# Three 256-column matmuls per weight tile in place of a 512- and a 256-column one, in a two-layer float32 transformer kernel

## The chip, the cores and the metric

One core of one Trainium2 chip. The metric is the device time of one launch in microseconds (us), the median of several runs.

## What is computed

Two layers over 256 tokens of 2048 channels, batch 1, all in float32. Each layer normalises, runs a mixer and adds it to the residual stream `h`, then normalises, runs a squared-ReLU MLP and adds that; a last norm follows. Cut to what matters here:

```python
# layer 0: even_mixer, layer 1: odd_mixer
hn  = rms_norm(h, norm_mix[layer])
h   = h + mixer(hn)          # hn @ w_in -> attention / recurrence -> @ w_out
hn  = rms_norm(h, norm_mlp[layer])
h   = h + jnp.square(jax.nn.relu(hn @ w_up[layer])) @ w_down[layer]
# at the end
out = rms_norm(h, final_norm)
```

The weights are 2048 x 3584 (even in), 2048 x 2048 (even out), 2048 x 6144 (odd in), 2048 x 2048 (odd out), and for each layer's MLP 2048 x 8192 and 8192 x 2048. Nearly all the work is these products.

## The kernel before, in words

**Split operands.** Every operand of a large product is held as a sum of two parts in the type float32r: a high part (a float32r copy) and a low part (the value minus that copy). The product then is high x high + high x low + low x high. For activations the two parts lie side by side in one row of `hg_op` (the normed stream) or `ff_op` (the mixer's or MLP's inner activations): columns 0 to 255 (S = 256 tokens) hold the high part, 256 to 511 the low one.

**Weights.** A weight slice of 512 rows x 256 columns (512 KB, [128, 4, 256] in SBUF) is one *sub*. `load_quad` (L327) has SyncE load a sub into one of four `raw` slots as soon as VectorE is done with the slot (`lo_done`). ScalarE makes the high part (`split_hi`, L338, the copy is L346), VectorE the low part (`split_lo`, L348, the subtraction is L353), both `AHEAD` = 3 subs ahead of TensorE, into one of four `w_split` slots.

**Quads.** Eight subs make a *quad*: 512 output columns as two groups of 256, each over the 2048 rows in four subs. There are 91 quads, so 728 subs. A quad's four output tiles of 128 channels x 256 tokens lie in PSUM banks 0 to 3, one tile a bank. `quad_pe` (L516) runs `pe_sub` (L355) for each sub: for each of the 2 output tiles and each of 4 row tiles it issues two matmuls (L374), so 8 pairs a sub, 5,824 pairs in all:

- "hi": weight tile high x the full 512-column row of the activations. High x high adds into columns 0 to 255 of the bank, high x low into columns 256 to 511 (the *cross half*).
- "lo": weight tile low x the 256 high columns, added into columns 0 to 255.

Each matmul is recorded as two instructions, a weight load (128 x 128, the row PEld) and the matmul. The order is lo, hi, but hi, lo for the first row tile of an output tile; so at row tiles 0 and 1 two 256-column matmuls stand side by side. Four quads of the odd mixer's input (its values, tokens on the partitions) go through `pe_sub_tok` (L381), where the activations are the stationary operand and the weights move; the same two widths, L401.

**Leaving PSUM.** `quad_split` (L523) is the order written out for ScalarE and VectorE: at each place 0 to 7 of a quad one split, and after the splits of places 4 and 7 (6 and 7 in quads with a late order) the group that is done *leaves*. First ScalarE waits for the tile (`pe_count`) and copies the cross half to SBUF (`act_cross`, L409, the copy is L412), then VectorE adds the main half to it into `total` (`dve_total`, L414, the add is L417) and frees the bank (`bank_free`). Then VectorE uses `total`: `residual` (L437) adds it into `h` (L463), `hidden` (L472) takes ReLU times the norm's factor (L485), `projected` (L492) scales it (L500). ScalarE and VectorE then make the next high and low parts. `projected_tok` (L502) folds the add into its scaling. TensorE waits for `bank_free` at the first sub of a group before it writes the bank again.

**Between them**, hooks of `stage_hook` put the attention, the recurrence, the norms and the final transposes at fixed places of the quads, on banks 4 to 7. VectorE's `h_ready` and `proj_done` tell them when `h` or a projection is there; `v_pe_stage` has TensorE transpose the first projection at place 2 of quad 1.

Of the kernel before, what the change touches and what calls it, by code (L numbers as in the profile page):

```python
# [36 lines left out]
P = 128  # L37
# [4 lines left out]
KT = 16  # L42
# [53 lines left out]
def build(nc, x, rel_bias, norm_mix, even_w_in, even_conv_w, even_conv_b, even_gate_a_w, even_gate_a_b,  # L96
# [30 lines left out]
    with ctx:  # L127
# [13 lines left out]
        cross = sb("cross", [P, 4, S])  # L141
        total = sb("total", [P, 4, S])
# [80 lines left out]
        cross_done = sem("cross_done")  # L223
        bank_free = sem("bank_free")
        relu_done = sem("relu_done")
# [10 lines left out]
        proj_done = sem("proj_done")  # L236
# [70 lines left out]
        R_EVEN_OUT, R_MLP0 = 0, 4  # L307
        R_ODD_OUT, R_MLP1 = 4 + 4 * CHUNKS, 8 + 4 * CHUNKS
# [46 lines left out]
        def pe_sub(pe, Q, s, pos, op, ready, base, first):  # L355

            g, kq = s // 4, s % 4
            slot = pos % SPLIT_SLOTS
            pe.wait_ge(lo_done, 8 * Q + pos + 1)
            if first:  # L360

                n = SUB_KT * (kq + 1)
                pe.wait_ge(ready, even_out_tiles(n) if isinstance(Q, int) and Q == Q_EVEN_OUT else base + n)
            for j in range(2):
                i = 2 * g + j
                if kq == 0 and not (isinstance(Q, int) and Q == 0):

                    pe.wait_ge(bank_free, 4 * Q - 4 + i + 1)
                for kt in range(SUB_KT):
                    k = SUB_KT * kq + kt  # L370
                    hi = (psum[:, i, 0:2 * S], w_hi[:, slot, kt, j * P:(j + 1) * P], op[:, k, :])
                    lo = (psum[:, i, 0:S], w_lo[:, slot, kt, j * P:(j + 1) * P], op[:, k, 0:S])
                    for n, (o, l, r) in enumerate((hi, lo) if k == 0 else (lo, hi)):
                        ins = nc.tensor.matmul(o, l, r, start=(k == 0 and n == 0), stop=(k == KT - 1 and n == 1),  # L374
                                               skip_group_check=True)
                if kq == 3:
                    ins.then_inc(pe_count, 1)
            if kq < 3:
                ins.then_inc(pe_count, 1)

        def pe_sub_tok(pe, Q, s, pos, op, ready, base, first):  # L381
# [8 lines left out]
            for tb in range(TB):  # L390
                i = 2 * g + tb
                if kq == 0:

                    pe.wait_ge(bank_free, 4 * Q - 4 + i + 1)
                both = psum[:, i].rearrange("p (a c) -> p a c", a=2)
                for kt in range(SUB_KT):
                    k = SUB_KT * kq + kt
                    hi = (both, op[:, k, tb * P:(tb + 1) * P], w_split[:, slot, :, kt, :])
                    lo = (both[:, 1], op[:, k, S + tb * P:S + (tb + 1) * P], w_hi[:, slot, kt, :])
                    for n, (o, l, r) in enumerate((hi, lo) if k == 0 else (lo, hi)):  # L400
                        ins = nc.tensor.matmul(o, l, r, start=(k == 0 and n == 0), stop=(k == KT - 1 and n == 1),  # L401
                                               skip_group_check=True)
                if kq == 3:
                    ins.then_inc(pe_count, 1)
# [14 lines left out]
        def act_prep(act, nrm, n, i, src_ready, col):  # L419

            act.wait_ge(h_ready, src_ready)
# [15 lines left out]
        def residual(which, eng, Q, g, R, n0, prep):  # L437
# [5 lines left out]
            if which == "act":  # L443
                act_cross(eng, Q, g)
                for i in tiles:
                    if last:
                        eng.wait_ge(h_ready, KT + 4 * R + i + 1)
                        eng.activation(sq[:, i], tile(h, n0 + i, 0, S), ACT.Square).then_inc(prep_done, 1)
                    elif prep:
                        act_prep(eng, prep[0], n0 + i, i, KT + 4 * R + i + 1, prep[1])  # L450
# [21 lines left out]
        def hidden(which, eng, Q, g, U, n0):  # L472

            if which == "act":
                act_cross(eng, Q, g)
                for i in (2 * g, 2 * g + 1):
                    eng.wait_ge(relu_done, 4 * U + i + 1)
# [4 lines left out]
            dve_total(eng, Q, g)  # L482
# [9 lines left out]
        def projected(which, eng, Q, g, dst, scale):  # L492

            if which == "act":
                act_cross(eng, Q, g)
                return
            dve_total(eng, Q, g)
            for i in (2 * g, 2 * g + 1):
                eng.wait_ge(bank_free, 4 * Q + i + 1)
                eng.scalar_tensor_tensor(dst(i), total[:, i], scale, rstd, ALU.mult, ALU.mult).then_inc(proj_done, 1)  # L500

        def projected_tok(which, eng, Q, g, c0):  # L502

            for tb in range(TB):
                i, r = 2 * g + tb, rstd_tok[:, tb:tb + 1]
                if which == "act":
                    eng.wait_ge(pe_count, after_tile(Q, i))
                    eng.wait_ge(rstd_done, 2 + 1)
                    eng.activation(cross[:, i], psum[:, i, S:2 * S], ACT.Copy, scale=r).then_inc(cross_done, 1)
                else:  # L510
                    eng.wait_ge(cross_done, 4 * Q + i + 1)
                    eng.scalar_tensor_tensor(v_tok[:, tb, c0:c0 + GC], psum[:, i, 0:S], r, cross[:, i],
                                             ALU.mult, ALU.add).then_inc(bank_free, 1)
# [282 lines left out]
        def kpad_act(act):  # L796
            act.wait_ge(proj_done, 2)
# [6 lines left out]
        def v_pe_stage(pe):  # L804
            pe.wait_ge(proj_done, 4)
# [17 lines left out]
        def swa_qk_pe(pe, g):  # L823
            key = SWA_FIRST[g]
            pe.wait_ge(proj_done, 4 * (1 + g // 2) + 2 * (g % 2) + 2)
# [114 lines left out]
        def lru_conv_dve(dve, m, taps):  # L940
            if taps[0] == 3:
                p0 = 4 * (3 + m // 2) + 2 * (m % 2)
                dve.wait_ge(proj_done, p0 + 2)
# [72 lines left out]
        def lru_out_act(act, m):  # L1016
            act.wait_ge(proj_done, 4 * (5 + m // 2) + 2 * (m % 2) + 2)
# [59 lines left out]
        def even_in_leave(Q):  # L1077
            q = Q - Q_EVEN_IN

            def leave(which, eng, g):  # L1080
# [12 lines left out]
                elif q <= 4:  # L1093
                    if which == "dve" and q == 3 and g == 0:
                        eng.memset(xpad[:, :, 0:3], 0.0).then_inc(dve_seq, 1)
                        seq["dve"] += 1
                        eng.wait_ge(dve_seq, seq["dve"])

# [13 lines left out]
        def z_pe(pe, n):  # L1112
            i = n % 4
            pe.wait_ge(proj_done, 4 * (7 + 4 + n // 4) + i + 1)
# [112 lines left out]
        def mixer_out(which, eng, w, Q0, R0, base, nrm, first_quad, key0):  # L1227
            for n in range(4):
                def leave(which, eng, g, n=n):
                    residual(which, eng, Q0 + n, g, R0 + n, 4 * n, (nrm, norm_cols[nrm]))  # L1230
# [3 lines left out]
        def mlp(which, eng, layer, Q0, R0, A0, nrm):  # L1234
# [10 lines left out]
            def down(c, g, prep=None, until=8, hook=None):  # L1245
                Q = Q0 + 8 * c + 4 + g
                run_quad(which, eng, Q, wd, D * c, 512 * g, ff_op, ff_ready, A0 + KT * c + 0,
                         lambda which, eng, grp: residual(which, eng, Q, grp, R0 + 4 * c + g, 4 * g, prep),
# [27 lines left out]
        def program(which, eng):  # L1276
            mixer_in(which, eng, w_even_in, Q_EVEN_IN, EVEN_IN_COLS, even_in_leave, 0, 0)
            mixer_out(which, eng, w_even_out, Q_EVEN_OUT, R_EVEN_OUT, A_EVEN, 1, Q_EVEN_IN, 0)
            mlp(which, eng, 0, Q_MLP0, R_MLP0, A_MLP0, 1)
            mixer_in(which, eng, w_odd_in, Q_ODD_IN, ODD_IN_COLS, odd_in_leave, 2, ODD)  # L1280
            mixer_out(which, eng, w_odd_out, Q_ODD_OUT, R_ODD_OUT, A_ODD, 3, Q_ODD_IN, ODD)
            mlp(which, eng, 1, Q_MLP1, R_MLP1, A_MLP1, 3)
# [155 lines left out]
```

## Time and profile before

| | |
|---|---|
| median of 3 runs | 2204.99 us (2204.65 to 2206.67) |
| the profiled execution, span from first to last instruction | 2204.3 us |
| the profiled execution's own time beside its span | not shown apart; the median of the runs is 0.7 us over the span |
| TensorE busy | 2147.9 us, 97% |
| TensorE weight loads busy | 1864.1 us, 85% |
| VectorE busy | 1328.2 us, 60% |
| ScalarE busy | 1139.4 us, 52% |
| granted TensorE clock, mean | 0.989 |
| moved by DMA | 392.83 MB, 178 GB/s |

A matmul's recorded duration includes the way through the array, and the records of neighbours overlap, so a duration isn't what the matmul costs. What it costs is the time from its start to the next one's: the length of an unbroken stretch over the number of matmuls in it.

### The profile page before, as it was taken

The page shows a single profiled execution, that of the slowest core. Times are in us where ns is not written, and L with a number is a line of the kernel's source. Part 1 is how long each engine was busy: PE and PEld are TensorE (multiplying, and loading weights), DVE is VectorE, ACT ScalarE, POOL GpSimd, SP SyncE. Part 2 cuts the span into 40 slices and gives each one's busy share as a digit, 9 for nine tenths or more (in the row PEclk, how much of TensorE's full clock was granted, in tenths as well). Part 3 has the DMA queues.
Part 4 walks back from the last instruction along what each step waited for, and adds up shares of the span by engine and source line. Part 5 has one row for each costly group of instructions (what it writes and reads, how often), then busy time and mean ns, then how long its engine had stood idle before and what let it go on. Part 6 is the DMA issues. An engine that isn't in the chain of part 4 may idle for free.

```text
span 2204.3 us, 34808 instructions
## 1 busy us (share of the span) xinstructions
PE 2147.9 (97%) x12170; PEld 1864.1 (85%) x12170; DVE 1328.2 (60%) x1873; ACT 1139.4 (52%) x1761; POOL 59.3 (3%) x91
## 2 busy tenths in 40 slices
PE   7499999999999999999999999999999999999998
PEld 6388888888888888888888888888888888888887
DVE  6268776655655665666655555676556656655664
ACT  4258855544544544555444466555445544544555
POOL 5011100000000000000000000000000000000000
PEclk9699999999999999999999999999999999999999
DMA  7854556566666566565555544556666656565653
GB/s 183 158 173 134 164 183 183 181 195 186 186 186 186 180 193 184 181 191 186 185 185 188 186 140 134 161 177 188 191 184 188 189 183 185 183 191 176 196 182 124
DMA packets 391821, 392.83 MB, mean 178 GB/s; under 512 B 15744, under 2 KB 388624, under 8 KB 391744
## 3 DMA queue, kind: packets, MB, share of 16 engines
q1 hardware_dynamic: 387552, 385.99, 56.7%
q0 software_dynamic: 3584, 5.79, 2.0%
q8 instruction: 48, 0.79, 0.2%
q14 instruction: 29, 0.24, 0.0%
q10 hardware_dynamic: 608, 0.03, 0.0%
HBM read 386.49 MB, written 5.24 MB: 178 GB/s over the span
## 4 chain that ended last, share of the span: by engine, by line
PE 95%; DMA 2%; ACT 1%; SPq 1%; DVE 0%; POOL 0%; issue 0%; ACTq 0%; DVEq 0%; POOLq 0%
PE psum L374 87%; PE psum L401 4%; DMA raw<-in_even_w_in_dram 2%; PE psum L837 0%; PE psum L1121 0%; POOL relu_sq L891 0%; PE psum L1147 0%; PE psum L1163 0%; PE psum L971 0%; PE psum L834 0%; SPq L579 0%; PE psum L1149 0%; DVE w_split L353 0%; PE psum L1165 0%; PE psum L1148 0%
## 5 line engine op out<-in xcount | busy, mean ns | idle before, releaser
L353 DVE TENSOR_TENSOR w_split<-raw,w_split 128x1024 fp32r<-128x1024 f32 x728 | 885.9, 1228 | 688.6 <-ACT w_split L346 684.5
L346 ACT ACTIVATE w_split<-raw 128x1024 fp32r<-128x1024 f32 x728 | 762.6, 1056 | 767.8 <-PE psum L374 679.8
L374 PE MATMUL psum<-hg_op,w_split 128*128 128x512 f32 (+1 forms) x6016 | 1078.0, 341 | 18.4 <-DVE w_split L353 18.1
L374 PEld LDWEIGHTS psum<-hg_op,w_split 128*128 128x128 f32 x6016 | 927.4, 189 | 158.8 <-DVE w_split L353 18.9
L374 PE MATMUL psum<-ff_op,w_split 128*128 128x512 f32 (+1 forms) x5120 | 907.1, 340 | 0.0
L374 PEld LDWEIGHTS psum<-ff_op,w_split 128*128 128x128 f32 x5120 | 785.1, 188 | 117.6
L412 ACT ACTIVATE cross<-psum 128x256 f32<-128x256 f32 x348 | 122.2, 377 | 124.6 <-PE psum L374 124.5
L417 DVE TENSOR_TENSOR total<-psum,cross 128x256 f32<-128x256 f32 x348 | 138.0, 418 | 58.8 <-ACT cross L412 58.6
L478 ACT ACTIVATE relu_sq<-relu_sq 128x256 f32<-128x256 f32 x128 | 52.5, 410 | 82.7 <-DVE relu_sq L485 82.7
L401 PE MATMUL psum<-w_split,hg_op 128*128 128x512 f32 (+1 forms) x512 | 90.7, 340 | 0.0
L401 PEld LDWEIGHTS psum<-w_split,hg_op 128*128 128x128 f32 x512 | 78.5, 188 | 11.8
L488 DVE TENSOR_TENSOR ff_op<-relu_sq,ff_op 128x256 f32 (+1 forms) x128 | 54.5, 426 | 54.4 <-ACT ff_op L479 52.6
L463 DVE TENSOR_TENSOR h<-h,total 128x256 f32 (+1 forms) x160 | 59.9, 416 | 0.1
L479 ACT ACTIVATE ff_op<-relu_sq 128x256 f32 (+1 forms) x128 | 51.4, 402 | 0.0
L485 DVE SCALAR_TENSOR_TENSOR relu_sq<-total,rstd 128x256 f32<-128x256 f32 x128 | 47.9, 416 | 0.0
L422 ACT ACTIVATE relu_sq<-h 128x256 f32<-128x256 f32 (+1 forms) x48 | 19.7, 410 | 31.9 <-DVE h L463 31.9
L432 DVE TENSOR_TENSOR ssq<-ssq,relu_sq 128x256 f32<-128x256 f32 x48 | 20.2, 421 | 14.7 <-ACT hg_op L423 14.7
L423 ACT ACTIVATE hg_op<-h,pcol 128x256 fp32r<-128x256 f32 (+1 forms) x48 | 23.7, 495 | 0.0
L500 DVE SCALAR_TENSOR_TENSOR mix<-total,rstd 128x256 f32<-128x256 f32 x60 | 23.7, 436 | 0.0
L433 DVE SCALAR_TENSOR_TENSOR hg_op<-h,pcol,hg_op 128x256 fp32r<-128x256 f32 (+1 forms) x48 | 22.9, 478 | 0.0
L834 PE MATMUL psum<-mix 128*128 128x128 f32 x32 | 5.3, 319 | 13.3 <-DVE mix L500 13.2
L1139 DVE SCALAR_TENSOR_TENSOR mix<-psum,mix 128x384 f32<-128x384 f32 x16 | 8.9, 558 | 14.4 <-ACT mix L1134 14.4
(150 smaller groups left out, 535.5 us busy)
## 6 DMA issues: line engine op xcount, KB each, us to landing
raw<-in_w_up_dram SPq DMA_DIRECT2D x256, 512.0 KB, 3.9
raw<-in_w_down_dram SPq DMA_DIRECT2D x256, 512.0 KB, 3.6
raw<-in_odd_w_in_dram SPq DMA_DIRECT2D x96, 512.0 KB, 3.5
raw<-in_even_w_in_dram SPq DMA_DIRECT2D x56, 512.0 KB, 4.4
raw<-in_even_w_out_dram SPq DMA_DIRECT2D x32, 512.0 KB, 4.3
raw<-in_odd_w_out_dram SPq DMA_DIRECT2D x32, 512.0 KB, 3.7
rel_dram<-mix POOLq DMA_DIRECT2D x4, 768.0 KB, 37.7
mix<-in_x_dram SPq DMA_DIRECT2D x4, 512.0 KB, 8.3
```

Of the source, the lines that this page charges most:

```text
L346: act.activation(w_hi[:, slot], raw[:, rs], ACT.Copy).then_inc(hi_done, 1)
L353: dve.tensor_tensor(w_lo[:, slot], raw[:, rs], w_hi[:, slot].bitcast(F32), ALU.subtract).then_inc(lo_done, 1)
L374: ins = nc.tensor.matmul(o, l, r, start=(k == 0 and n == 0), stop=(k == KT - 1 and n == 1), skip_group_check=True)
L401: ins = nc.tensor.matmul(o, l, r, start=(k == 0 and n == 0), stop=(k == KT - 1 and n == 1), skip_group_check=True)
L412: act.activation(cross[:, i], psum[:, i, S:2 * S], ACT.Copy).then_inc(cross_done, 1)
L417: dve.tensor_tensor(total[:, i], psum[:, i, 0:S], cross[:, i], ALU.add).then_inc(bank_free, 1)
L423: act.activation(tile(hg_op, n, 0, S), tile(h, n, 0, S), ACT.Copy, scale=pcol[:, 0, one(col + n)]).then_inc(prep_done, 1)
L463: eng.tensor_tensor(dst, dst, total[:, i], ALU.add).then_inc(h_ready, 1)
L478: eng.activation(sq[:, i], relu[:, i], ACT.Square).then_inc(sq_done, 1)
L479: eng.activation(tile(ff_op, n0 + i, 0, S), relu[:, i], ACT.Square).then_inc(sq_done, 1)
L485: eng.scalar_tensor_tensor(relu[:, i], total[:, i], 0.0, rstd, ALU.max, ALU.mult).then_inc(relu_done, 1)
L488: eng.tensor_tensor(tile(ff_op, n0 + i, S, 2 * S), sq[:, i], tile(ff_op, n0 + i, 0, S).bitcast(F32), ALU.subtract).then_inc(ff_ready, 1)
```

## The change

In `pe_sub` and `pe_sub_tok` the 512-column matmul becomes two of 256 columns that load the same stationary tile again, and all three of a row tile add into columns 0 to 255 of the bank. The cross half, the copy of it by ScalarE and the add by VectorE are gone, with the buffers `cross` and `total`. VectorE waits for `pe_count` itself and reads PSUM where it read `total`; `bank_free` is now signalled by that consumer and takes the place of `h_ready`, `relu_done` and `proj_done` for those who waited for them. `projected_tok` becomes one scaling on VectorE. One wait is new in the even mixer: before VectorE writes `xpad` again it waits for the convolution, which it runs itself.

```diff
@@ pe_sub
+                acc = psum[:, i, 0:S]
                 for kt in range(SUB_KT):
                     k = SUB_KT * kq + kt
-                    hi = (psum[:, i, 0:2 * S], w_hi[:, slot, kt, j * P:(j + 1) * P], op[:, k, :])
-                    lo = (psum[:, i, 0:S], w_lo[:, slot, kt, j * P:(j + 1) * P], op[:, k, 0:S])
-                    for n, (o, l, r) in enumerate((hi, lo) if k == 0 else (lo, hi)):
-                        ins = nc.tensor.matmul(o, l, r, start=(k == 0 and n == 0), stop=(k == KT - 1 and n == 1),
-                                               skip_group_check=True)
+                    wh, wl = w_hi[:, slot, kt, j * P:(j + 1) * P], w_lo[:, slot, kt, j * P:(j + 1) * P]
+                    nc.tensor.matmul(acc, wl, op[:, k, 0:S], start=(k == 0), stop=False)
+                    nc.tensor.matmul(acc, wh, op[:, k, S:2 * S], start=False, stop=False)
+                    ins = nc.tensor.matmul(acc, wh, op[:, k, 0:S], start=False, stop=(k == KT - 1))
@@ pe_sub_tok
-                both = psum[:, i].rearrange("p (a c) -> p a c", a=2)
+                acc = psum[:, i, 0:GC]
-                    hi = (both, op[:, k, tb * P:(tb + 1) * P], w_split[:, slot, :, kt, :])
-                    lo = (both[:, 1], op[:, k, S + tb * P:S + (tb + 1) * P], w_hi[:, slot, kt, :])
+                    ah, al = op[:, k, tb * P:(tb + 1) * P], op[:, k, S + tb * P:S + (tb + 1) * P]
+                    nc.tensor.matmul(acc, al, w_hi[:, slot, kt, :], start=(k == 0), stop=False)
+                    nc.tensor.matmul(acc, ah, w_lo[:, slot, kt, :], start=False, stop=False)
+                    ins = nc.tensor.matmul(acc, ah, w_hi[:, slot, kt, :], start=False, stop=(k == KT - 1))
@@ gone
-        def act_cross(act, Q, g):
-            for i in (2 * g, 2 * g + 1):
-                act.wait_ge(pe_count, after_tile(Q, i))
-                act.activation(cross[:, i], psum[:, i, S:2 * S], ACT.Copy).then_inc(cross_done, 1)
-        def dve_total(dve, Q, g):
-            for i in (2 * g, 2 * g + 1):
-                dve.wait_ge(cross_done, 4 * Q + i + 1)
-                dve.tensor_tensor(total[:, i], psum[:, i, 0:S], cross[:, i], ALU.add).then_inc(bank_free, 1)
@@ residual, VectorE
-            dve_total(eng, Q, g)
             for i in tiles:
-                eng.wait_ge(bank_free, 4 * Q + i + 1)
+                eng.wait_ge(pe_count, after_tile(Q, i))
                 dst = tile(h, n0 + i, 0, S)
-                eng.tensor_tensor(dst, dst, total[:, i], ALU.add).then_inc(h_ready, 1)
+                eng.tensor_tensor(dst, dst, psum[:, i, 0:S], ALU.add).then_inc(bank_free, 1)
@@ hidden, VectorE (projected likewise, with its own scaling)
-                eng.wait_ge(bank_free, 4 * Q + i + 1)
-                eng.scalar_tensor_tensor(relu[:, i], total[:, i], 0.0, rstd, ALU.max, ALU.mult).then_inc(relu_done, 1)
+                eng.wait_ge(pe_count, after_tile(Q, i))
+                eng.scalar_tensor_tensor(relu[:, i], psum[:, i, 0:S], 0.0, rstd, ALU.max, ALU.mult).then_inc(bank_free, 1)
@@ even_in_leave, VectorE, for xpad
+                        if q > 3 or g:
+                            eng.wait_ge(lru_xc, 2 * (2 * (q - 3) + g))
```

## Rows read from the trace of the kernel before

**Rows 1.** The page: busy time by engine, and the granted clock in 40 slices.

```profile
PE 2147.9 (97%) x12170; PEld 1864.1 (85%) x12170; DVE 1328.2 (60%) x1873; ACT 1139.4 (52%) x1761; POOL 59.3 (3%) x91
PEclk9699999999999999999999999999999999999999
```

**Rows 2.** Windows by stage: busy of each engine (instructions), clock, DMA share, GB/s.

```profile
core 0: us, PE busy (x) PEld busy (x) DVE busy (x) ACT busy (x) POOL busy (x), PEclk, DMA share, GB/s
0.00:100.00 100.00, 55.94 (x270) 47.55 (x271) 44.65 (x59) 38.05 (x60) 34.66 (x66) 0.80 0.84 180
350.00:1075.00 725.00, 725.00 (x4112) 629.78 (x4111) 441.11 (x612) 363.48 (x547) 0.00 (x0) 1.00 0.60 186
2192.50:2204.30 11.80, 1.42 (x9) 0.99 (x8) 4.07 (x11) 5.14 (x11) 0.00 (x0) 0.64 0.47 178
```

**Rows 3.** The chain of waits, 400 to 1060 us: start us, us, what.

```profile
399.94 660.29 PE psum L374 x3742
```

**Rows 4.** Groups of TensorE instructions by line and shape.

```profile
L374 PE MATMUL psum<-ff_op,w_split 128*128 128x512 f32 x2560 | 893.8, 398 | 0.0
L374 PE MATMUL psum<-ff_op,w_split 128*128 128x256 f32 x2560 | 693.6, 281 | 0.0
...
L374 PEld LDWEIGHTS psum<-ff_op,w_split 128*128 128x128 f32 x5120 | 785.1, 188 | 117.6
```

**Rows 5.** The chain of waits while the granted clock was 0.50, with that window.

```profile
33.61 4.27 PE psum L374 x13
...
33.82:37.68 3.86, 3.86 (x14) 3.26 (x13) 3.86 (x4) 1.20 (x2) 3.27 (x3) 0.50 0.73 223
```

**Rows 6.** Timeline at row tiles 0 and 1: matmuls 256, 256, 512; weight loads.

```profile
807.62 0.63 PE L374 MATMUL psum<-ff_op,w_split 128*128 128x256 f32 x3
...
807.62 0.30 PEld L374 LDWEIGHTS psum<-ff_op,w_split 128*128 128x128 f32 x2
...
807.74 0.31 PEld L374 LDWEIGHTS psum<-ff_op,w_split 128*128 128x128 f32 x2
```

**Rows 7.** Timeline at the end: four matmuls with a single moving column each.

```profile
2195.22 0.52 PEld L1328 LDWEIGHTS psum<-ones,ssq 128*128 128x128 f32 x4 [3.02 <-DVE ssq L468]
```

**Rows 8.** The chain of waits: plain float32 matmuls, 128 columns (L905), 512 columns (L915).

```profile
122.83 0.87 PE psum L905 x8
...
126.48 0.86 PE psum L915 x2
```

**Rows 9.** The page: groups of ScalarE and VectorE instructions that the change touches.

```profile
L412 ACT ACTIVATE cross<-psum 128x256 f32<-128x256 f32 x348 | 122.2, 377 | 124.6 <-PE psum L374 124.5
L417 DVE TENSOR_TENSOR total<-psum,cross 128x256 f32<-128x256 f32 x348 | 138.0, 418 | 58.8 <-ACT cross L412 58.6
...
L463 DVE TENSOR_TENSOR h<-h,total 128x256 f32 (+1 forms) x160 | 59.9, 416 | 0.1
```

**Rows 10.** Who waited for whom: line <- releaser: us, times, longest.

```profile
ACT w_split L346 <- PE psum L374: 679.8, 429, 7.7
...
PE psum L374 <- DVE w_split L353: 18.1, 2, 17.0
PE psum L834 <- DVE mix L500: 13.2, 1, 13.2
```

**Rows 11.** The chain of waits at the end of quad 0 and before L834.

```profile
45.13 0.39 ACT cross L412
45.52 0.02 issue
45.54 0.42 DVE total L417
45.97 0.67 DVE mix L500 x2
46.63 1.15 DVE w_split L353
...
47.80 40.82 DMA raw<-in_even_w_in_dram
...
92.86 0.67 DVE total L417 x2
93.53 0.68 DVE mix L500 x2
```

**Rows 12.** The chain of waits behind the last large matmul.

```profile
2189.74 2.80 PE psum L374 x16
2192.54 0.02 issue
2192.56 0.39 ACT cross L412
2192.95 0.02 issue
2192.98 0.42 DVE total L417
2193.40 0.34 DVE h L463
```

More of the change, by code:

```diff
@@ L140, in build @@
         ff_op = sb("ff_op", [P, KT, 2 * S], F32R)
-        cross = sb("cross", [P, 4, S])
-        total = sb("total", [P, 4, S])
         relu_sq = sb("relu_sq", [P, 8, S])
@@ L406, in pe_sub_tok, with act_prep @@
                 ins.then_inc(pe_count, 1)
[L409 to L421 removed]
+        def act_prep(act, nrm, n, i, count, col):
+            act.wait_ge(bank_free, count)
             act.activation(sq[:, i], tile(h, n, 0, S), ACT.Square).then_inc(prep_done, 1)
@@ L435, in dve_prep, with residual @@
                                      ALU.mult, ALU.subtract).then_inc(hg_ready, 1)
-        def residual(which, eng, Q, g, R, n0, prep):
+        def residual(which, eng, Q, g, n0, prep):
             tiles = (2 * g, 2 * g + 1)
@@ L494, in projected @@
             if which == "act":
-                act_cross(eng, Q, g)
                 return
-            dve_total(eng, Q, g)
             for i in (2 * g, 2 * g + 1):
-                eng.wait_ge(bank_free, 4 * Q + i + 1)
-                eng.scalar_tensor_tensor(dst(i), total[:, i], scale, rstd, ALU.mult, ALU.mult).then_inc(proj_done, 1)
+                eng.wait_ge(pe_count, after_tile(Q, i))
+                eng.scalar_tensor_tensor(dst(i), psum[:, i, 0:S], scale, rstd, ALU.mult, ALU.mult).then_inc(bank_free, 1)
         def projected_tok(which, eng, Q, g, c0):
+            if which == "act":
+                return
             for tb in range(TB):
                 i, r = 2 * g + tb, rstd_tok[:, tb:tb + 1]
[L506 to L513, printed above, removed]
+                eng.wait_ge(pe_count, after_tile(Q, i))
+                eng.wait_ge(rstd_done, 2 + 1)
+                eng.tensor_scalar(v_tok[:, tb, c0:c0 + GC], psum[:, i, 0:GC], r, None, ALU.mult).then_inc(bank_free, 1)
         def quad_pe(pe, Q, op, ready, base, hook=None):
@@ L804, in v_pe_stage @@
         def v_pe_stage(pe):
[L805 removed]
+            pe.wait_ge(bank_free, 4)
             for m in range(2):
@@ L1097, in leave @@
                         eng.wait_ge(dve_seq, seq["dve"])
+                    if which == "dve":
+                        if q > 3 or g:
+                            eng.wait_ge(lru_xc, 2 * (2 * (q - 3) + g))
                     def dst(i):
@@ L1247, in down @@
                 run_quad(which, eng, Q, wd, D * c, 512 * g, ff_op, ff_ready, A0 + KT * c + 0,
-                         lambda which, eng, grp: residual(which, eng, Q, grp, R0 + 4 * c + g, 4 * g, prep),
+                         lambda which, eng, grp: residual(which, eng, Q, grp, 4 * g, prep),
                          hook, until)
@@ L1277, in program @@
             mixer_in(which, eng, w_even_in, Q_EVEN_IN, EVEN_IN_COLS, even_in_leave, 0, 0)
-            mixer_out(which, eng, w_even_out, Q_EVEN_OUT, R_EVEN_OUT, A_EVEN, 1, Q_EVEN_IN, 0)
-            mlp(which, eng, 0, Q_MLP0, R_MLP0, A_MLP0, 1)
+            mixer_out(which, eng, w_even_out, Q_EVEN_OUT, A_EVEN, 1, Q_EVEN_IN, 0)
+            mlp(which, eng, 0, Q_MLP0, A_MLP0, 1)
             mixer_in(which, eng, w_odd_in, Q_ODD_IN, ODD_IN_COLS, odd_in_leave, 2, ODD)
-            mixer_out(which, eng, w_odd_out, Q_ODD_OUT, R_ODD_OUT, A_ODD, 3, Q_ODD_IN, ODD)
-            mlp(which, eng, 1, Q_MLP1, R_MLP1, A_MLP1, 3)
+            mixer_out(which, eng, w_odd_out, Q_ODD_OUT, A_ODD, 3, Q_ODD_IN, ODD)
+            mlp(which, eng, 1, Q_MLP1, A_MLP1, 3)
         def fin_pe_group(pe, G, grp, first=False, banks=None):
```

33 lines of the change are left out of this document (11 added, 22 removed).

## The prediction

> **What bounds the kernel now.** I read the page first. TensorE is busy 97% of the span, VectorE 60%, ScalarE 52%, and the granted clock is full (2.4 GHz) after the start [rows 1]. The windows by stage show where the missing 3% lie: in the first 100 us TensorE works 56 us, in the 725 us from 350 on it has no gap, in the last 12 us it does almost nothing [rows 2]. The list of waits confirms it: ScalarE waits 680 us for TensorE to free a split slot, TensorE waits for a split twice, 18 us together, at the start [rows 10]. So the time is the pace of the main matmuls plus a start and an end, and the question is what a triple of 256-column matmuls takes against a pair of 512 and 256.
>
> The pace comes from an unbroken stretch: 3,742 matmuls in 660.29 us are 176.45 ns each, **352.9 ns a pair** [rows 3]. A pair moves 768 columns, 320 ns at 2.4 GHz, so a pair pays 32.9 ns above its columns: 0.4595 ns a column where the clock would give 0.4167. While the clock was at 1.2 GHz the same code took 4.27 us for 13 matmuls, seven of 512 and six of 256 columns, 5,120 columns; 5,120 / 1.2 is 4.27 us [rows 5]. There the excess is nothing, and the weight loads cost nothing either. The recorded durations, 398 and 281 ns [rows 4], overlap and are no price.
>
> **The change part by part.**
>
> *Matmuls.* 768 moving columns before and after, but 5,824 more matmuls and as many more weight loads. Of the 728 subs (8 pairs each) 11 run before the first transposes of quad 1 at 94 us, in a stretch that waits for weights and not for TensorE; 717 x 8 = 5,736 pairs run at TensorE's pace. Each nanosecond on a row tile is 5.7 us.
>
> What does a 256-column matmul with its own weight load take among its like? The trace has the case, once for each output tile, where two such stand side by side. Starting at 807.62 the timeline has 256, 256, 512 columns in 0.63 us; less the 0.40 us record of the 512 [rows 4] the two took **0.23 us, 115 ns each**. The weight loads tell the same: two of them span 0.30 us, the next two 0.31 us, each load is a 0.19 us record, so they started 0.11 and 0.12 us apart [rows 6]. Both neighbours write the same half bank, from different weights, which is what the new kernel does throughout. The other value is the rate per column, 256 x 0.4595 = 117.6 ns. I take the middle, **116 ns**, since the side-by-side row is the exact case but only two long, and the rate is long but of mixed widths. A triple is 348 ns, 4.9 ns less than the pair: 4.9 x 5,736 = **-28 us**.
>
> *Bounds of that term.* Below: a load cannot be hidden under less than itself. With one moving column each, four loads span 0.52 us, so (0.52 - 0.19) / 3 = 110 ns from load to load [rows 7]. Three times 110 is 330 ns, -23 ns a triple, -131 us; nothing in the trace suggests that the excess vanishes so wholly. With the shorter of the two gaps, 0.30 us less a record of 188 ns [rows 4, 6] or 112 ns, a triple is 336 ns and the term -97 us. Above: if the whole 32.9 ns of excess came with the matmuls and not with the columns, 16.4 ns each, the triple would be 369.4 ns, +16.4 x 5,736 = +94 us.
>
> *The load, by row and by rule.* Rows 6 have loads 0.11 and 0.12 us apart with 256 columns streaming the while, so load and stream overlap almost wholly. The Trainium skill, page "TensorE: Matmul & The Clock Gate", section "The mechanism", says that a weight load overlaps matmuls in flight only where the row group differs; here it never does. By that rule a third load, which the same page's section "LDWEIGHTS" prices at its column count over 1.2 GHz, an estimated 107 ns, would add some 600 us. The trace disagrees: two loads and 768 columns in 352.9 ns leave no room for it.
>
> *ScalarE and VectorE.* 348 copies (122 us) and 348 adds (138 us) go [rows 9]. Both lie beside TensorE, so in the steady part they are worth nothing; their absence lowers VectorE from 60% towards 54%. The add into `h` takes 416 ns from SBUF, the add that reads PSUM 418 ns [rows 9], so consumers keep their price. VectorE now waits for TensorE itself at place 7, for the quad's last sub. Queued behind are the next quad's splits, but three subs lie split ahead, 3 x 8 x 352.9 ns = 8.5 us, against a few operations of 0.4 us; and the old path had the same wait one engine earlier. If that cover went, TensorE would stall once a quad. The bank is freed after one operation of VectorE in place of two on two engines, four subs before it is wanted. The new wait on the convolution is for VectorE's own earlier work: nothing.
>
> *Start.* At the end of quad 0 the copy and one add stand in the chain, 0.39 + 0.42 us, but a 40.8 us load of weights follows, in the crowded first stretch, which may or may not come earlier: 0 to -0.8, I take -0.4. Ahead of the transposes at 94 us two adds, 0.67 us, stand in the chain [rows 11]; ScalarE's copies there ran beside a split. -0.7 us.
>
> *End.* Behind the last matmul the copy and the add, 0.02 + 0.39 + 0.02 + 0.42 us, fall out; the last add into `h` then runs whole, 0.42 instead of 0.34 [rows 9, 12]. -0.8 us.
>
> *Transfers.* Faster by 1.4%, TensorE wants 186 GB/s to be 189, at a DMA share of 0.60 [rows 2]. Nothing.
>
> Sum: -28 - 0.4 - 0.7 - 0.8 = -30 us. Against the profiled span of 2204.3 us that is 2174.4; the median of the runs lies 0.7 us above the span, so **2175 us**.
>
> **The rivals.**
>
> *Nothing but the ends* (column rate). If TensorE pays 0.4595 ns per column whatever the widths, the triple is 352.9 ns and only the 2 us go: 2203 us. For it: one sum of columns gives one time, and in rows 6 the load gap of 0.12 us agrees with 117.6 ns. Against: 0.23 us for the two is below 235 ns, though only just.
>
> *The full gain.* 112 ns throughout, -97 - 2: 2106 us. For it: the shorter gap of rows 6. Against: the longer one beside it.
>
> *A price per matmul* (the other side). Each matmul and its load cost something fixed, and the change adds one to each row tile. Its lower price comes from plain float32 matmuls: 128 columns take 0.87 / 8 = 109 ns, 512 columns 0.86 / 2 = 430 ns [rows 8]; the line through both has 1.7 ns left at zero columns, +10 us and with the ends 2213. Its upper price is the +94 above: 2297. It decides from 117.6 ns per 256-column matmul on, where three cost more than the pair. Against the upper price: two 256 side by side would take 2 x 123 = 246 ns, and rows 6 show 230. But no row has more than two such in succession, and a reserve that two loads draw on and three exhaust would look just like this. The Trainium skill gives such a floor too: "TensorE: Matmul & The Clock Gate", section "Back-to-back issue gap", has 2.5 ns a matmul beyond its columns at full clock, which for one more each is an estimated +14 us; the rows' 1.7 ns agrees in size.
>
> *The change doesn't do what it says.* A consumer in PSUM could hold a bank longer and stall TensorE. It is freed by one 0.4 us operation; I give it no chance of its own.
>
> **How the numbers follow.** A measurement of this kernel can tell about 0.2%, 4.4 us, from no change. Gain of some size (348 ns and the full gain together): 0.60, of which the triple near 348 has most. Column rate: 0.15. Price per matmul: 0.25. Likeliest is the gain near 348 ns: 2175. Its own range runs from 2140 to 2200. For 8 in 10 the range must reach into the other side, past the lower price at 2213 and part of the way to 2297, for a fixed cost up to about 5.5 ns a matmul: 2235. Below it reaches most of the way to the full gain, 2122, 113.4 ns a matmul. Left out are the far part of the price per matmul, about 0.12, and what lies below 2122, about 0.08.
>
> **What the profile after would show.** An unbroken stretch of L-lines for the main matmuls: right if its length over its count is near 116 ns, between 113 and 117.4; wrong if over 117.6. Twice 5,824 = 11,648 becomes 17,472 main matmuls. No groups for the cross copy and the total; ScalarE near 1,017 us, VectorE near 1,190. At the end the last matmul to the first of the small ones should be 2.7 us less 0.8. What would make it wrong: a row tile whose three matmuls take unequal times, the third the longest (a reserve used up), or waits of TensorE for VectorE's splits that weren't there.

## The result and the profile after

The change makes the kernel slower: **2243.56 us** median (2243.43 to 2243.69) against 2204.95 us for the kernel before in the same session, a ratio of 1.0175, interval 1.0163 to 1.0187. That is +38.6 us where -30 was forecast, and above the top of the range (2235).

The page of the changed kernel, busy time by engine:

```profile
span 2241.6 us, 45567 instructions
...
PE 2190.3 (98%) x17994; PEld 2176.8 (97%) x17994; DVE 1219.5 (54%) x1525; ACT 1030.2 (46%) x1397; POOL 59.2 (3%) x91
```

Against [rows 1], the matmuls are there as announced (12,170 became 17,994), VectorE and ScalarE are relieved as announced, and TensorE is busy for 42 us more. The weight loads' busy time is the line to stop at: 97% of the span instead of 85%. Loads now follow each other so closely that their records overlap all the time.

The windows and the timelines of the changed kernel (windows: us, busy and instructions of PE, PEld, DVE, ACT, POOL, then clock, DMA share, GB/s; timelines: start us, us, what):

```profile
400.00:1000.00 600.00, 600.00 (x5002) 600.00 (x5001) 315.58 (x369) 256.34 (x321) 0.00 (x0) 1.00 0.59 182
```

```profile
599.96 0.19 PEld L366 LDWEIGHTS psum<-hg_op,w_split 128*128 128x128 f32 x1
600.08 0.19 PEld L367 LDWEIGHTS psum<-hg_op,w_split 128*128 128x128 f32 x1
600.20 0.19 PEld L368 LDWEIGHTS psum<-hg_op,w_split 128*128 128x128 f32 x1
...
33.14 0.41 PE L367 MATMUL psum<-hg_op,w_split 128*128 128x256 f32 x1
33.36 0.41 PE L368 MATMUL psum<-hg_op,w_split 128*128 128x256 f32 x1
33.57 0.41 PE L366 MATMUL psum<-hg_op,w_split 128*128 128x256 f32 x1
```

```profile
33.90:37.60 3.70, 3.70 (x19) 3.70 (x19) 3.70 (x5) 0.22 (x1) 3.38 (x4) 0.50 0.54 163
```

A window's count takes in the records that reach over its edges, two more than fit: at the pace of [rows 3] 600 us hold 3,400 matmuls, and before's window shows 3,402. So the pace after is 600 us / 5,000 = **120.0 ns** a matmul, 360.0 ns a row tile against 352.9. The timeline says it plainly, a load every 0.12 us, all three lines alike. It is 13.3 ns more than 256 columns take at 2.4 GHz. In the early stretch with a granted clock of 0.50, 1.2 GHz, the matmuls start 0.21 us apart, 256 / 1.2 = 213 ns: there, as in [rows 5], nothing is paid over the columns.

Start and end in the chain of waits of the changed kernel (start us, us, what):

```profile
90.44 1.23 DVE w_split L346
91.67 0.68 DVE mix L476 x2
92.39 2.07 PE psum L807 x8
...
2230.49 0.13 PE psum L368
2230.62 0.02 issue
2230.64 0.43 DVE h L443
2231.07 0.02 issue
2231.09 0.42 ACT relu_sq L429
2231.52 0.02 issue
2231.54 0.43 DVE ssq L448
2231.98 0.04 issue
2232.02 0.62 PE psum L1304 x4
```

The same places in the kernel before, and TensorE's wait for GpSimd in the attention, before and after (last two lines: us, times, longest):

```profile
94.25 2.07 PE psum L834 x8
...
2194.22 0.44 DVE ssq L468
...
2194.75 0.44 DVE ssq L468
...
2195.23 0.62 PE psum L1328 x4
...
PE psum L901 <- POOL relu_sq L891: 1.9, 2, 1.0
...
PE psum L874 <- POOL relu_sq L864: 0.7, 1, 0.7
```

The transposes start at 92.4 us instead of 94.25, and from the last large matmul to the small ones it is 1.4 us instead of 2.7 [rows 12]: -3.2 us in all. The account of the span: +7.1 ns x 5,736 row tiles = +40.7, less 3.2, is +37.5; measured 2241.6 - 2204.3 = +37.3. (The profiled execution took 2243.43 us.) That it comes out so closely is partly luck. The wait in the attention falls by another 1.2 us, and what follows the first small matmul takes 0.4 us longer.

The end is sure: 1.4 us in all four kernels here that leave out the copy and the add, 2.7 or more in all the others. The start is not. Among the kernels that keep the copy and the add, the transposes start anywhere from 91.92 (e12) to 94.51 us (e10), among the four without them from 92.29 to 93.43. So one trace of each can't tell how much of the 1.9 us the change earned.

### The profile page after: what moved, and what is told of

The parts are those of the page before. It is cut to its first block, busy times and chain, and to the rows that moved or that the text cites. A ratio compares the mean times of both kernels' runs of the same rounds, so it can differ in the third digit from the quotient of the medians.

```text
span 2241.6 us, 45567 instructions
## 1 busy us (share of the span) xinstructions
PE 2190.3 (98%) x17994; PEld 2176.8 (97%) x17994; DVE 1219.5 (54%) x1525; ACT 1030.2 (46%) x1397; POOL 59.2 (3%) x91
## 4 chain that ended last, share of the span: by engine, by line
PE 96%; DMA 2%; SPq 0%; ACT 0%; DVE 0%; POOL 0%; issue 0%; ACTq 0%; DVEq 0%; POOLq 0%
PE psum L366 29%; PE psum L368 29%; PE psum L367 29%; DMA raw<-in_even_w_in_dram 2%; PE psum L392 1%; PE psum L393 1%; PE psum L394 1%; PE psum L1097 0%; PE psum L810 0%; PE psum L1123 0%; PE psum L1139 0%; PE psum L944 0%; PE psum L807 0%; POOL relu_sq L864 0%; SPq L552 0%
## 5 line engine op out<-in xcount | busy, mean ns | idle before, releaser
L346 DVE TENSOR_TENSOR w_split<-raw,w_split 128x1024 fp32r<-128x1024 f32 x728 | 895.3, 1231 | 871.1 <-ACT w_split L339 868.9
L366 PE MATMUL psum<-hg_op,w_split 128*128 128x256 f32 x3008 | 859.2, 286 | 18.3 <-DVE w_split L346 18.1
L367 PE MATMUL psum<-hg_op,w_split 128*128 128x256 f32 x3008 | 853.7, 284 | 0.0
L368 PE MATMUL psum<-hg_op,w_split 128*128 128x256 f32 x3008 | 853.6, 284 | 0.0
L366 PE MATMUL psum<-ff_op,w_split 128*128 128x256 f32 x2560 | 725.4, 283 | 0.0
L368 PE MATMUL psum<-ff_op,w_split 128*128 128x256 f32 x2560 | 724.4, 283 | 0.0
L367 PE MATMUL psum<-ff_op,w_split 128*128 128x256 f32 x2560 | 724.4, 283 | 0.0
L366 PEld LDWEIGHTS psum<-hg_op,w_split 128*128 128x128 f32 x3008 | 579.9, 193 | 20.3 <-DVE w_split L346 18.5
L367 PEld LDWEIGHTS psum<-hg_op,w_split 128*128 128x128 f32 x3008 | 580.0, 193 | 1.2 <-issue 1.0
L368 PEld LDWEIGHTS psum<-hg_op,w_split 128*128 128x128 f32 x3008 | 579.9, 193 | 0.0
L367 PEld LDWEIGHTS psum<-ff_op,w_split 128*128 128x128 f32 x2560 | 491.5, 192 | 0.0
L366 PEld LDWEIGHTS psum<-ff_op,w_split 128*128 128x128 f32 x2560 | 491.5, 192 | 0.0
L368 PEld LDWEIGHTS psum<-ff_op,w_split 128*128 128x128 f32 x2560 | 491.4, 192 | 0.0
L443 DVE TENSOR_TENSOR h<-h,psum 128x256 f32 (+1 forms) x160 | 63.2, 416 | 20.7 <-PE psum L368 20.7
L392 PE MATMUL psum<-w_split,hg_op 128*128 128x256 f32 x256 | 72.5, 283 | 0.0
L393 PE MATMUL psum<-w_split,hg_op 128*128 128x256 f32 x256 | 72.4, 283 | 0.0
L394 PE MATMUL psum<-w_split,hg_op 128*128 128x256 f32 x256 | 72.4, 283 | 0.0
L463 DVE SCALAR_TENSOR_TENSOR relu_sq<-psum,rstd 128x256 f32<-128x256 f32 x128 | 50.8, 418 | 7.2 <-PE psum L368 7.2
```

Of the source, the lines that this page charges most:

```text
L346: dve.tensor_tensor(w_lo[:, slot], raw[:, rs], w_hi[:, slot].bitcast(F32), ALU.subtract).then_inc(lo_done, 1)
L366: nc.tensor.matmul(acc, wl, op[:, k, 0:S], start=(k == 0), stop=False)
L367: nc.tensor.matmul(acc, wh, op[:, k, S:2 * S], start=False, stop=False)
L368: ins = nc.tensor.matmul(acc, wh, op[:, k, 0:S], start=False, stop=(k == KT - 1))
L392: nc.tensor.matmul(acc, al, w_hi[:, slot, kt, :], start=(k == 0), stop=False)
L393: nc.tensor.matmul(acc, ah, w_lo[:, slot, kt, :], start=False, stop=False)
```

## The experiments

"Pace" is 600 us over the count less two, in the window from 400 to 1,000 us; for each kernel its row of the windows is shown, with the columns as above. Those with one number for their time have one run. Beside it stands one run of the kernel before (2203.68 us for e5 to e8, 2204.95 for e13 to e15) or, for e9, e10 and e12, seven (median 2204.90); differences of a few us in them are not read. e1 to e4 change the four token-major quads too, the experiments from e5 on leave them as they are, hence the 5,480 row tiles in their expectations. The diffs show the deciding lines, with arguments left out (`...`) and, in e1 and e2, a comment for the lines taken out.

### The two halves of the change, each alone

`e1_three_with_cross`: before, with the matmuls in three.

```diff
-                    # hi: 512 columns into [0:2S], lo: 256 into [0:S]
+                    nc.tensor.matmul(psum[:, i, 0:S], wl, op[:, k, 0:S], ...)
+                    nc.tensor.matmul(psum[:, i, S:2 * S], wh, op[:, k, S:2 * S], ...)
+                    ins = nc.tensor.matmul(psum[:, i, 0:S], wh, op[:, k, 0:S], ...)
```

> The change's three 256-column matmuls alone: the high x low one still adds into the cross half of the bank, and the copy by ScalarE and the add by VectorE stay as before. Theory A (each float32r matmul with its weight load pays 13.3 ns over its columns at full clock, so the triple is 360 ns wherever its outputs lie): 120 ns a matmul, and the 2 us of the start and end are not gained: 2205 + 7.1 x 5736 ns = 2246 us. Rival B (the slowness comes from three adds in a row into the same half bank): the two halves take turns here, so the triple is at or under the pair's 352.9 ns and the time near 2205 us or less.

```profile
400.00:1000.00 600.00, 600.00 (x5002) 600.00 (x5002) 348.75 (x473) 288.17 (x425) 0.00 (x0) 1.00 0.58 182
```

2246.57 us, ratio 1.0187 (1.0170 to 1.0204): 120.0 ns with the outputs in both halves of the bank. Rival B falls: the one half bank costs nothing.

`e2_pairs_without_cross`: the changed kernel with before's two matmuls.

```diff
-                    # three 256-column matmuls into [0:S]
+                    hi = (psum[:, i, 0:2 * S], w_hi[...], op[:, k, :])
+                    lo = (psum[:, i, 0:S], w_lo[...], op[:, k, 0:S])
```

> The other half of the change alone: before's 512- and 256-column matmuls, with the copy and add gone and the consumers reading the main half in PSUM, as in the changed kernel. The high x low term is computed but left out of the result. All theories that put the loss into the matmuls: pace of 176.45 ns a matmul as before, and only the start and the end gain, 2 us: 2203 us. Rival C (VectorE's new wait on the matmuls or the later freeing of banks costs TensorE time): over 2206 us, with waits of TensorE that before does not have.

```profile
400.00:1000.00 600.00, 600.00 (x3402) 521.16 (x3401) 325.11 (x385) 263.18 (x333) 0.00 (x0) 1.00 0.61 186
```

2201.54 us, ratio 0.9984 (0.9974 to 0.9993): before's pace and -3.4 us. In the traces (spans 2199.9 and 2204.3 us) e2 is 3.2 us ahead at 224 us, at the 768th main matmul, and still 3.2 us at the last one; the end adds 1.3. So nothing is gained in the stretch where TensorE has no gap. The new wait of VectorE costs TensorE nothing; rival C falls. The halves add up: +41.6 and -3.4 are +38.2 of the 38.6 us.

### Is the price one of columns, of matmuls or of loads?

`e5_both_512`, `e7_two_of_384` and `e8_four_matmuls`:

```diff
 # e5, on before
-                    lo = (psum[:, i, 0:S], w_lo[...], op[:, k, 0:S])
+                    lo = (psum[:, i, 0:2 * S], w_lo[...], op[:, k, :])
 # e7, on before
+                    hi = (psum[:, i, 0:384], w_hi[...], op[:, k, 0:384])
+                    lo = (psum[:, i, 0:384], w_lo[...], op[:, k, 0:384])
 # e8, on the changed kernel
-                    nc.tensor.matmul(acc, wh, op[:, k, S:2 * S], ...)
+                    for c in (0, P):
+                        nc.tensor.matmul(psum[:, i, c:c + P], wh, op[:, k, S + c:S + c + P], ...)
```

> Before, with the low matmul 512 columns wide too, so that low x low adds into the cross half: all main matmuls of 512 columns (the four token-major quads stay as before). The alternate order gave 233 ns for a 512-column matmul that follows another one, and the change 120 ns for a 256-column one; a straight line through these, theory F (6.7 ns a matmul and 0.4427 ns a column), says 233.3 ns each throughout, 466.7 ns a pair, +113.8 x 5480 ns: 2829 us. Theory A as first put (13.3 ns a matmul, nothing by column): 226.7 ns each, 2755 us.

```profile
400.00:1000.00 600.00, 600.00 (x2651) 496.89 (x2650) 283.46 (x387) 235.19 (x351) 0.00 (x0) 1.00 0.46 144
```

> Before, with two matmuls of 384 columns per row tile in place of 512 and 256: same number of matmuls, same sum of columns, one width throughout. The result is not the reference's: the high x low term covers only the first 128 tokens, low x low is added there, and the copy by ScalarE takes columns 128 to 383. Theory F (6.7 ns a matmul, 0.4427 ns a column): 176.7 ns each, 353.3 ns a pair: 2207 us. Theory A as first put (13.3 ns a matmul): 173.3 ns each, -6.2 x 5480 ns: 2171 us. If the 349.1 ns of the alternate order came from equal widths standing together, one width throughout should also give 349 or less: 2183 us.

```profile
400.00:1000.00 600.00, 600.00 (x3463) 600.00 (x3462) 364.50 (x499) 299.36 (x445) 0.00 (x0) 1.00 0.60 189
```

> The changed kernel, with the high x low matmul cut once more into two of 128 columns, each with its load: four matmuls, the same 768 columns, the right result. Theory F carried on below 256 columns: 6.7 ns for one more, 366.7 ns a row tile, +37 us: 2281 us. Theory L (a load takes 110 ns or more from one to the next, as before's matmuls with one moving column show, and cannot hide behind 128 columns): 120 + 112 + 112 + 120 = 464 ns or a little more, +104 x 5480 ns: 2814 us.

```profile
400.00:1000.00 600.00, 600.00 (x5180) 599.95 (x5180) 249.25 (x297) 205.09 (x264) 0.00 (x0) 1.00 0.46 142
```

Times 2755.68, 2174.72 and 2805.19 us. With 512 columns throughout the pace is 226.5 ns, with 384 it is 173.4, with 256 it was 120.0. Less the columns at 2.4 GHz (213.3, 160.0, 106.7) that leaves **13.2, 13.4 and 13.3 ns: a fixed price, whatever the width.** Theory F, the line I had drawn meanwhile through mixed widths, falls; my first form of theory A holds. Nor does the price follow the traffic beside it: e5 had it with 144 GB/s and VectorE 47% busy, e7 with 189 GB/s and 61%. At 128 columns another bound takes over: 115.9 ns a matmul on the average of four, 463.5 ns a row tile, as theory L had it (464). The loads of a row tile in e8:

```profile
600.04 0.19 PEld L366 LDWEIGHTS psum<-ff_op,w_split 128*128 128x128 f32 x1
600.16 0.31 PEld L368 LDWEIGHTS psum<-ff_op,w_split 128*128 128x128 f32 x2
600.39 0.19 PEld L370 LDWEIGHTS psum<-ff_op,w_split 128*128 128x128 f32 x1
600.51 0.19 PEld L366 LDWEIGHTS psum<-ff_op,w_split 128*128 128x128 f32 x1
```

They start 0.11 to 0.12 us apart, no closer than [rows 7] show (0.11), though two of the four matmuls have only 128 columns.

`e6_loads_of_64`, on the changed kernel, asks whose the 13.3 ns are:

```diff
+                    m = P if k in (0, KT - 1) else P // 2
+                    acc = psum[0:m, i, 0:S]
-                    wh, wl = w_hi[:, slot, kt, j * P:(j + 1) * P], w_lo[:, slot, kt, j * P:(j + 1) * P]
+                    wh, wl = w_hi[:, slot, kt, j * P:j * P + m], w_lo[:, slot, kt, j * P:j * P + m]
```

> The changed kernel, with weight loads of 64 columns in place of 128 for all row tiles but the first and the last of an output tile; half the output channels miss 14 of 16 row tiles, so the result is not the reference's. It asks whether the excess of a 256-column matmul (13.3 ns) belongs to its load. If all of it is the load's, by the load's columns: 113.3 ns each, -6.7 x 3 x 5480 x 7/8 ns = -96 us: 2148 us. If only the part per matmul (6.7 ns) is: 116.7 ns each, 2196 us. If it is the matmul's own or the stream's: 120 ns each and 2244 us.

```profile
400.00:1000.00 600.00, 600.00 (x5248) 600.00 (x5247) 335.61 (x399) 270.39 (x343) 0.00 (x0) 1.00 0.60 192
```

2155.24 us. The pace is 114.4 ns with one load in eight still full; with those at 120.0 the others come to (114.4 - 15.0) / 0.875 = 113.6 ns, where half of 13.3 over the columns would be 113.3. **The price goes with the columns of the stationary tile.** The edit halves the load, but also the output partitions that the matmul writes, and no run here has a matmul without a load of its own. So that the load is what is paid for is the likely reading, not a shown one.

### Why before's pair costs 352.9 ns and not 346.7

Two loads at 13.3 ns over 320 ns make 346.7. The pair pays 6.2 ns more. Two runs changed only the order of before's matmuls:

```diff
 # e3
-                    for n, (o, l, r) in enumerate((hi, lo) if k == 0 else (lo, hi)):
+                    for n, (o, l, r) in enumerate((hi, lo) if k % 2 == 0 else (lo, hi)):
 # e4
+                for n in range(2):              # the four hi of an output tile, then its four lo
+                    for kt in range(SUB_KT):
```

> Before, with high and low matmuls in the order hi, lo, lo, hi, hi, lo, lo, hi by row tile, so that widths change half as often. Same work, same result up to the order of the sums. Theory A with a second term (13.3 ns a matmul, and 3.3 ns each time the width changes, which makes up before's 352.9 ns): one change a pair in place of two, 349.9 ns a pair, -17 us: 2188 us. Rival D (before's 32.9 ns are paid by column, 0.4595 ns each, and the change's loss is a price of the third load only): no change, 2205 us. Rival E (the order matters through the half bank: a 512-column matmul that follows a 256-column one into the same half waits for it): also 2188 or so, and then grouping in the next run gives no more per change removed.

```profile
400.00:1000.00 600.00, 600.00 (x3446) 523.48 (x3446) 362.74 (x496) 297.82 (x442) 0.00 (x0) 1.00 0.61 188
```

> Before, with the four 512-column matmuls of an output tile first in each sub and then its four of 256 columns: two changes of width in eight matmuls in place of eight. Theory A with the second term: 346.7 + 2 x 3.3 / 4 = 348.3 ns a pair, -26 us: 2179 us; within a group 226.7 ns from a 512-column matmul to the next and 120 ns from a 256-column one to the next. Rival D: no change, 2205 us.

```profile
400.00:1000.00 600.00, 600.00 (x3423) 524.37 (x3422) 360.48 (x495) 297.08 (x440) 0.00 (x0) 1.00 0.60 186
```

The alternate order: 2182.68 us, ratio **0.9898** (0.9881 to 0.9914), 174.2 ns a matmul, 348.4 a pair. The grouped one: 2194.86 us, 0.9954 (0.9937 to 0.9971), 350.8 a pair. So order matters, but the second term of theory A, a price for each change of width, is wrong: the grouped order has the fewest changes and is the slower of the two. Rival D falls as well. (The expectations quoted around here give 349.1 ns for the alternate order, a value per column in which I counted some matmuls with the wrong width; the window's count gives 348.4. For 448 and 320 columns it gives 347.0, not 346.9.)

`e11_tiles_in_turn` keeps the widths 512, 512, 256, 256 and has neighbours of a width write the two output tiles in turn:

```diff
+                for n, j in ((0, 0), (0, 1), (1, 0), (1, 1)):
+                    i = 2 * g + j
```

> By now 13.3 ns a load holds wherever one width runs throughout (256, 384, 512 columns), so a pair should cost 346.7 ns; before's pair costs 352.9 and the alternate order's 349.1, so mixing widths costs 6.2 or 2.4 ns. This run has the width sequence of the alternate order (512, 512, 256, 256), the right result, but neighbours of one width write the two tiles of a group in turn, so no matmul adds into the bank that the one before it wrote, but for the change from 512 to 512 of the next row tile. If the mixing price is one of the width sequence (theory W): 349.1 ns a pair and 2183 us, as the alternate order. If it is one of adding into the same bank just written (theory E): 346.7 ns and 2169 us. Over 2190 us would be a price of changing banks.

```profile
400.00:1000.00 600.00, 600.00 (x3447) 523.49 (x3446) 361.31 (x494) 295.42 (x443) 0.00 (x0) 1.00 0.60 188
```

2183.12 us, ratio 0.9901 (0.9885 to 0.9918): the same as the alternate order, so it is the sequence of widths and not the bank written before. (The loop goes hi, hi, lo, lo over the tiles 0, 1, 0, 1, so no two neighbours at all share a bank.)

`e9_low_reads_second_half` and `e12_same_weights` move one operand of the low matmul:

```diff
-                    lo = (psum[:, i, 0:S], w_lo[...], op[:, k, 0:S])
+                    lo = (psum[:, i, 0:S], w_lo[...], op[:, k, S:2 * S])   # e9
+                    lo = (psum[:, i, 0:S], w_hi[...], op[:, k, 0:S])       # e12
```

> Before, with the low matmul reading the second 256 columns of the activations' row (low x low in place of low x high, so the result lacks a term): same widths, same order, another address for one moving operand. If the mixing price comes from where the moving operand lies (theory M): a clearly different pace, 346.7 ns a pair and 2170 us at best. If not: 352.9 ns, 2205 us.

> Before, with the low matmul loading the high weights (the result has high x high twice and lacks low x high): same widths and order, but two neighbouring loads read the same tile, as two of the three do in the changed kernel. If where the loads read matters (theory M again): a different pace, down to 2170 us. If not: 352.9 ns, 2205 us.

2206.19 and 2204.87 us, counts of 3,403 and 3,402: before's pace. Theory M falls.

`e10_448_and_320` and `e15_480_and_288` change the widths at the same sum:

```diff
+                    hi = (psum[:, i, 0:448], w_hi[...], op[:, k, 0:448])   # e15: 480
+                    lo = (psum[:, i, 0:320], w_lo[...], op[:, k, 0:320])   # e15: 288
```

> Before's order with 448 and 320 columns in place of 512 and 256: the same 768 columns in two matmuls, still two widths. The result is not the reference's (part of the high x low term is missing, part of low x low is added). Theory W (any change of width costs): about 352.9 ns a pair, 2205 us. Theory S (the price needs a matmul so short that the next load just fits behind it: 256 columns are 107 ns, a load 110, while 320 are 133 ns): 346.7 ns a pair as with two of 384, 2173 us.

```profile
400.00:1000.00 600.00, 600.00 (x3460) 572.53 (x3459) 363.81 (x497) 299.14 (x445) 0.00 (x0) 1.00 0.60 189
```

> Before's order with 480 and 288 columns (the result misses part of the high x low term and has part of low x low). 448 and 320 gave 346.9 ns a pair, so no price for mixing; 288 columns are 120 ns at full clock against 107 for 256. Theory S: a full load fits behind 120 ns, or all but: 346.7 to 348 ns, 2173 to 2180 us. Theory R: the price stays or falls in proportion, to about 350 ns, 2188 us.

```profile
400.00:1000.00 600.00, 600.00 (x3455) 552.19 (x3454) 363.01 (x496) 299.12 (x444) 0.00 (x0) 1.00 0.60 189
```

2178.07 and 2179.83 us, 347.0 and 347.5 ns a pair, so mixing as such is almost free; of the three pairs of widths only 512 and 256 pays much for it. `e13` and `e14` shorten one load of before's pair in 14 of 16 row tiles, behind the narrow or behind the wide matmul:

```diff
+                    m = (P if k in (0, KT - 1) else P // 2)
+                    hi = (psum[0:m, i, 0:2 * S], w_hi[:, slot, kt, j * P:j * P + m], op[:, k, :])    # e13
+                    lo = (psum[0:m, i, 0:S], w_lo[:, slot, kt, j * P:j * P + m], op[:, k, 0:S])      # e14
```

> Before, with the load of the 512-column matmul, which runs while the 256-column one streams, cut to 64 columns in 14 of 16 row tiles (half the output channels miss those, so the result is not the reference's). A load costs 13.3 ns at 128 columns and half at 64. Theory S (before's other 6.2 ns a pair come from a full load that does not quite fit behind 256 columns): they go too, 320 + 13.3 + 6.7 = 340.0 ns a pair, -12.9 x 5480 x 7/8 = -62 us: 2142 us. Theory R (those 6.2 ns belong to the ratio of widths or to multiples of 256 as such): 346.2 ns, 2173 us.

```profile
400.00:1000.00 600.00, 600.00 (x3512) 529.80 (x3511) 370.91 (x511) 304.11 (x453) 0.00 (x0) 1.00 0.61 192
```

> The mirror of the run before it: the load of the 256-column matmul, which runs while the 512-column one streams, cut to 64 columns in 14 of 16 row tiles. There is room behind 512 columns anyway. Theory S: only the load's own half goes, 352.9 - 6.7 = 346.2 ns a pair, -32 us: 2173 us. If it is as fast as the run before it (2142 us), the place of the load does not matter and theory S falls.

```profile
400.00:1000.00 600.00, 600.00 (x3460) 455.20 (x3459) 363.74 (x498) 298.60 (x444) 0.00 (x0) 1.00 0.60 189
```

2148.90 and 2176.56 us. e13 has 341.9 ns a pair; with one pair in eight at 352.9, the others are at 340.3, where theory S said 340.0 and theory R 346.2. e14 has 347.0, or 346.2 for its short ones, as expected for half a load's price alone. **The 6.2 ns go when the wide matmul's stationary tile, which is loaded while the 256-column matmul streams, is halved; they stay when the narrow one's is.** They go as well, with full tiles, when the narrow matmul has 288 columns or more. Both point to the full load behind 256 columns; as in e6, the shorter tile also halves the output, so the load alone is not shown. What happens in the chip there is open too: in the changed kernel every load runs behind 256 columns and none pays more than 13.3 ns. Why a narrow matmul among wide ones does, and why 512, 512, 256, 256 brings it down to 1.7 ns, stays open.

## Why the prediction was wrong, step by step

- *What bounds the kernel*: right. TensorE is without a gap from 350 us on, before and after.
- *Matmuls*, the step that failed: "the two took 0.23 us, 115 ns each ... I take the middle, 116 ns". Measured: 120.0 ns, 360.0 a triple instead of 348, +40.7 us instead of -28. The term is a sum of two that the trace of before did not separate: a third matmul with its load, +13.3 ns, and the 6.2 ns of the pair that go, together +7.1.
- *Why that row misled*: it was read past what it can bear. In the trace, read to the nanosecond from 400 to 1,000 us, a 256-column matmul starts 113.4 ns ahead of another one and 117.3 ahead of a 512-column one, and a 512-column matmul 235.8 ns ahead of the next (most between 227 and 241), while e5 gives 226.5 for 512 columns and the change 120.0 for 256. Start times among mixed widths shift by several ns, so that two starts 0.23 us apart cannot decide about 4 ns between 116 and 120. What two narrow matmuls seem to save there, their wide neighbours pay. The loads were no second witness: in the trace each starts a few ns after a matmul does (both at 807.62 in [rows 6]). And the changed kernel's neighbours don't all load different weights, two of three load the same tile; e12 shows that this makes no difference.
- *The other value, the rate per column* (117.6 ns): wrong too. e5 pays 0.442 ns a column, e7 0.451, the changed kernel 0.469.
- *The load, by row and by rule*: "load and stream overlap almost wholly" is right, and a third load in full was never the danger. The "almost" was: each further matmul with its load costs 13.3 ns over its columns, 5,736 times. The Trainium skill's rule ("TensorE: Matmul & The Clock Gate", section "The mechanism") that a load in the same row group does not overlap doesn't hold here: three loads and 768 columns (320 ns) take 360.0 ns.
- *Bounds of that term*: right; +7.1 ns lies between -23 and +16.4. The upper one had the right idea, all the excess by the matmul and none by the column, and counted the pair's 6.2 ns in with it (16.4 ns each instead of 13.3).
- *Rival "a price per matmul"*: this is what happened, and it had 0.25. Its lower price, 1.7 ns from plain float32 matmuls [rows 8], says little of this case: those take 430 ns for 512 columns, twice the 213 of one column a cycle, and float32r pays nothing either while it moves a column in that time, at 1.2 GHz. Its objection ("two 256 side by side would take 2 x 123 = 246 ns") was the misreading above; "a reserve that two loads draw on and three exhaust" is not needed. The range ended at 5.5 ns a matmul where 7.1 net was paid.
- *The Trainium skill's floor* ("TensorE: Matmul & The Clock Gate", section "Back-to-back issue gap"), 2.5 ns a matmul, had the right sign; here each matmul has its own load of 128 columns and pays 13.3 ns.
- *ScalarE and VectorE, transfers*: right in what they are worth. There is no new wait of TensorE, and e2 shows the whole relief to be worth 3.4 us. The relief itself is smaller than forecast: VectorE 1219.5 us instead of some 1,190, ScalarE 1030.2 instead of 1,017.
- *Start and end*: the end fell by 1.3 us instead of 0.8. In before VectorE makes both totals of the last group ahead of either add into `h`, so the first tile is held up as well, and its add into `ssq` (0.44 us, at 2194.22) stands in the chain beside the second's (at 2194.75); after, one is left. The start is 1.9 us earlier instead of 1.1, which is within what the start of such kernels varies by. A place that the prediction did not have is the wait for GpSimd in the attention, 1.9 us before and 0.7 after.

## What to carry to other kernels

Where TensorE is the bound, price a split of a wide matmul by the matmuls with their loads that it adds, and take that price from a stretch of one width, or build one: a stretch of mixed widths gives one equation for two unknowns, and single start-to-start times in it are not the price of a width. Relief for engines that wait for TensorE is worth only what it takes off TensorE's own waits, here at the end, in the attention and perhaps at the start, 3.4 us together. The order of matmuls of two widths is free to choose and was worth 1%: before's kernel with the order hi, lo, lo, hi beats both versions, 2182.7 us.

## What the runs showed of the hardware

- A float32r matmul with its own load of 128 columns takes 13.3 ns more than its columns at 2.4 GHz, with 256, 384 or 512 moving columns alike, and about half as much more (6.9) with a stationary tile of 64 columns. At 1.2 GHz it takes no more than its columns (0.21 us for 256).
- Loads of 128 columns start no closer than 0.11 us between 400 and 1,000 us of e8, whose four matmuls of together 768 columns take 463.5 ns.
- 256 columns between 512-column neighbours pay a further 6.2 ns a pair; 320 and 448 pay 0.3, 288 and 480 pay 0.8, the order 512, 512, 256, 256 pays 1.7, and four of each in turn 4.1.
- Three adds in a row into the same PSUM columns pay nothing over adds into two halves in turn (120.0 ns both).
